# Gates of 128 of 256 tokens scattered by adding transfers instead of built by matmuls, in a one-core decoder step

## What is computed

```
q = (h @ w_q).reshape(C, 8, 2, 128)
s = einsum('cphd,phkd->cphk', q, sub_keys)
s1, i1 = top_k(s[:, :, 0], 16);  s2, i2 = top_k(s[:, :, 1], 16)
cand = s1[..., :, None] + s2[..., None, :]        # 16 x 16
top_s, top_i = top_k(cand, 16)
e = (i1 * 128 + i2) at top_i
g = softmax(top_s)
a = gelu(einsum('cpkd,cd->cpk', u_tab[e], h))
out = einsum('cpk,cpkd->cd', g * a, v_tab[e])
```

## Time and profile before

| | us |
|---|---|
| median of 3 runs | 1083.57 |
| runs | 1078.32, 1083.83, 1083.57 |
| the profiled execution | 1080.47 |
| its span | 1078.8 |

### The profile page before, as it was taken

One profiled execution on the slowest core, in us unless ns is written; L12 is line 12 of the kernel. 1 busy time (PEld: TensorE's weight loads), 2 busy tenths in 40 slices (PEclk: granted clock), 3 DMA queues, 4 the chain that ended last, 5 costly groups with the idle time before them and its releaser, 6 DMA issues.

```text
span 1078.8 us, 23502 instructions
## 1 busy us (share of the span) xinstructions
PE 1054.4 (98%) x7240; PEld 947.7 (88%) x7240; DVE 856.5 (79%) x1952; ACT 553.8 (51%) x1052; POOL 128.1 (12%) x151
## 2 busy tenths in 40 slices
PE   7999998999999999999999999999999999999997
PEld 7997647989999999999999999997788888888865
DVE  5324386698988989888459999987888888888878
ACT  5425475454544444444555555555555555555543
POOL 0344400000001000544000000000201001010100
PEclk9999999999999999999999999999999999999999
DMA  7655932333468766999864444558888888888872
GB/s 278 267 190 186 353 116 107 102 134 131 164 219 288 248 236 225 373 411 413 294 212 122 146 146 141 156 172 314 294 297 284 296 280 295 285 292 289 293 247 93
DMA packets 96248, 253.19 MB, mean 235 GB/s; under 512 B 11424, under 2 KB 44224, under 8 KB 95408
## 3 DMA queue, kind: packets, MB, share of 16 engines
q1 hardware_dynamic: 81840, 196.84, 52.5%
q0 software_dynamic: 14368, 55.87, 14.7%
HBM read 232.60 MB, written 22.12 MB: 236 GB/s over the span
## 4 chain that ended last, share of the span: by engine, by line
PE 81%; DMA 8%; DVE 5%; issue 3%; ACT 2%; SPq 1%; DVEq 0%; POOL 0%; ACTq 0%; POOLq 0%
PE ps L562 13%; PE ps L563 13%; PE ps L564 13%; PE ps L1039 9%; PE ps L1041 9%; PE ps L1040 9%; DMA activations<-u_out 5%; PE ps L1016 5%; DMA a_in<-activations 2%; PE ps L646 1%; DVE w_lo L1437 1%; PE ps L938 1%; ACT w_hi L1097 1%; DMA ring<-in_w_in_dram 1%; DMA vrow<-in_v_dram,expert 0%
## 5 line engine op out<-in xcount | busy, mean ns | idle before, releaser
L1437 DVE TENSOR_TENSOR w_lo<-ring,w_hi 128x512 fp32r<-128x512 f32 (+1 forms) x455 | 388.8, 858 | 124.0 <-ACT w_hi L1097 105.0
L1097 ACT CAST w_hi<-ring 128x512 fp32r<-128x512 f32 (+1 forms) x453 | 341.0, 753 | 96.7 <-PE ps L1041 60.8
L562 PE MATMUL ps<-h_hi,w_hi 128*128 128x256 f32 (+1 forms) x1128 | 330.3, 293 | 0.4 <-issue 0.2
L563 PE MATMUL ps<-h_lo,w_hi 128*128 128x256 f32 (+1 forms) x1128 | 321.1, 285 | 0.0
L564 PE MATMUL ps<-h_hi,w_lo 128*128 128x256 f32 (+1 forms) x1128 | 319.4, 283 | 0.0
L562 PEld LDWEIGHTS ps<-h_hi,w_hi 128*128 128x128 f32 x1128 | 214.9, 191 | 4.0 <-issue 3.2
L563 PEld LDWEIGHTS ps<-h_lo,w_hi 128*128 128x128 f32 x1128 | 214.2, 190 | 0.0
L564 PEld LDWEIGHTS ps<-h_hi,w_lo 128*128 128x128 f32 x1128 | 211.8, 188 | 0.0
L1039 PE MATMUL ps<-w_hi,y_hi 128*128 128x512 f32 x496 | 193.7, 391 | 2.2 <-DVE y_lo L1921 1.9
L1041 PE MATMUL ps<-w_lo,y_hi 128*128 128x512 f32 x496 | 193.0, 389 | 0.0
L1040 PE MATMUL ps<-w_hi,y_lo 128*128 128x512 f32 x496 | 193.0, 389 | 0.0
(11 more groups left out here) (372 smaller groups left out, 1278.6 us busy)
## 6 DMA issues: line engine op xcount, KB each, us to landing
ring<-in_uT_dram SPq DMA_DIRECT2D x128, 512.0 KB
ring<-in_v_dram SPq DMA_DIRECT2D x128, 512.0 KB
activations<-u_out SPq DMA_DIRECT2D x128, 128.0 KB
a_in<-activations SPq DMA_DIRECT2D x124, 128.0 KB, 4.6
ring<-in_w_in_dram SPq DMA_DIRECT2D x22, 512.0 KB
ring<-in_w_q_dram SPq DMA_DIRECT2D x16, 512.0 KB
ks<-in_cache_sb_dram POOLq DMA_DIRECT2D x16, 256.0 KB, 3.2
vs<-in_cache_sb_dram POOLq DMA_DIRECT2D x16, 256.0 KB, 5.5
```

Of the source, the lines that this page charges most:

```text
L562: mm(out, hi, hi_, start=start, stop=False)
L563: mm(out, hi, lo_, start=False, stop=False)
L1097: nc.scalar.copy(w_hi[slot][:, x], ring[:, ring_slot, x]).then_inc(part_hi, 2 if half is None else 1)
L1437: V.tensor_tensor(w_lo[slot][:, x], ring[:, ring_slot, x], w_hi[slot][:, x].bitcast(F32), ALU.subtract).then_inc(part_lo[ring_slot], 2 if ...
```

## The change

It does these things:

- The gates of tokens 0 to 127 no longer come from matmuls. Eight transfers on SP, after three w_out loads, write zeros over an 8 MB table in DRAM (`g_dram`, read as [first index, second index, token]). DVE computes for each of the 128 slots (8 heads x 16) of each token the position (first index x 128 + second index) x 128 + token, and the gate. POOL issues 128 indirect transfers, one for each slot, that add 128 single values (one for each token) to the table, with a wait for all that went before at each 16th. Eight transfers of 1 MB then bring the table into `gates[:, 0]`, each waiting for the one before, and the first for the end of up tile 111, since the buffers of the weights lie there.
- The gates of tokens 128 to 255 are built as before, in 16 up tiles instead of 32 (`U_ALONE` is 112).
- On DVE the lists of the first half are sorted first, then its route, then the samples, then the lists of the second half, four row products, its route, and the other 28 products, with five low parts more after each fourth. On POOL the gathers of u rows stand in groups of four between the scatters; the v gathers stand behind the eight loads.
- `hrow` is added to `sacc` by DVE instead of by PE.
- In front: `ns_turn` ahead of `rms_sums(0)`, five first halves of output tiles instead of four, one low part moved behind the last sums of the LayerNorm; at the end the samples' square root and finish are at other places.

The diff, without the lines that only allocate or assert:

```diff
 
-        U_ALONE = NE - DT // 8
+        U_ALONE = NE - GN // 8
 
...
         OUT_BANK = (4, 5, 6, 7, 0, 1, 2, 3)
-        OUT_DONE = [2 * AT_OUT + 4 + OUT_ORDER.index(c) + 1 if c < 4 else 2 * (AT_OUT + c + 1) for c in range(N_OUT)]
+        OUT_DONE = [2 * AT_OUT + 5 + OUT_ORDER.index(c) + 1 if c < 4 else 2 * (AT_OUT + c + 1) for c in range(N_OUT)]
 
...
                 load(AT_OUT + n, w_out[n])
+            sp.wait_ge(cmp_clear, 1)
+            for q in range(8):
+                sp.dma_start(g_rows[:, 16 * q:16 * (q + 1), :],
+                             spread_out[:, :].unsqueeze(1).to_broadcast([128, 16, 128])).then_inc(cleared, 16)
             sp.wait_ge(ss_pv, 2)
...
             pool.wait_ge(ch_mm, 2)
+            nc.gpsimd.memset(spread_out[:, :], 0.0)
             nc.gpsimd.memset(cvd[:, :], 0.0)
...
             at_slot = lambda k: bass.IndirectOffsetOnAxis(ap=expert[:, k:k + 1], axis=0)
-            pool.wait_ge(ix_ready, 1)
-            for k in range(SLOTS):
-                if k >= 4:
-                    pool.wait_ge(u_dot, k - 3)
-                nc.gpsimd.indirect_dma_start(urow[:, k % 4, :], None, u_rows, at_slot(k)).then_inc(ug_in[k % 4], 16)
+            def gates_out(first, last):
+                for m in range(first, last):
+                    if m and m % TOPK == 0:
+                        pool.wait_ge(spread_in, 16 * m)
+                    nc.gpsimd.indirect_dma_start(
+                        g_dram, bass.IndirectOffsetOnAxis(ap=spread_at[:, m:m + 1], axis=0), spread_out[:, m:m + 1],
+                        None, compute_op=ALU.add).then_inc(spread_in, 16)
+
+            def rows_in(first):
+                for k in range(first, first + 4):
+                    if k >= 4:
+                        pool.wait_ge(u_dot, k - 3)
+                    nc.gpsimd.indirect_dma_start(urow[:, k % 4, :], None, u_rows, at_slot(k)).then_inc(ug_in[k % 4], 16)
+
+            pool.wait_ge(cleared, 16 * 8)
+            pool.wait_ge(spread_ready, 1)
+            for part in range(16):
+                gates_out(8 * part, 8 * part + 8)
+                if part == 1:
+                    pool.wait_ge(ix_ready, 1)
+                    rows_in(0)
+                if part == 2:
+                    rows_in(4)
+                if 4 <= part < 10:
+                    rows_in(8 + 4 * (part - 4))
+            pool.wait_ge(spread_in, 16 * 8 * TOPK)
+            pool.wait_ge(w_mm, 2 * (AT_U + U_ALONE))
+            for q in range(8):
+                if q:
+                    pool.wait_ge(gates_in, 16 * q)
+                pool.dma_start(gates[:, 0, 16 * q:16 * (q + 1), :], g_rows[:, 16 * q:16 * (q + 1), :]).then_inc(gates_in, 16)
             v_rows = v.rearrange("j p d -> (j p) d")
...
             row_in(1, 1, None)
-            pool.wait_ge(g_sb, 4 + DT // 4)
+            pool.wait_ge(g_sb, 4 + GN // 4)
             for m in range(2, SLOTS):
...
                 if u == 7:
-                    rms_sums(0)
                     ns_turn()
...
                     np_values(u - 1)
+                if u == 7:
+                    rms_sums(0)
                 if u == 1:
...
             out_tile(2, range(4))
-            for c in OUT_ORDER[0:4]:
+            out_tile(4, range(4))
+            for c in OUT_ORDER[0:5]:
                 out_tile(c, range(4, KD))
-            for c in range(4, KD):
+            for c in range(5, KD):
                 out_tile(c, range(KD))
...
 
-            pe.wait_ge(rt_pick, 2)
+            pe.wait_ge(rt_pick, 1)
             pe.wait_ge(s_sb, 4 + 16)
...
             for c in range(3):
-                for tt, (t0, n) in enumerate(TOK[0:2]):
-                    ins = nc.tensor.transpose(ps[:, 4 + c, t0:t0 + n], pick[0:n, tt, c, :], ident[0:n, 0:n])
-                ins.then_inc(rt_t, 1)
+                nc.tensor.transpose(ps[:, 4 + c, 0:GN], pick[:, 1, c, :], ident[:, :]).then_inc(rt_t, 1)
             experts_up(U_ALONE // 4 - 1, U_ALONE // 4)
...
             pe.wait_ge(rt_slot, 3)
-            with pe.Fori(0, DT // 32) as i:
+            with pe.Fori(0, GN // 32) as i:
                 for r in range(4):
...
             ins.then_inc(f_mm, 1)
-            pe.wait_ge(g_sb, 4 + DT // 4)
+            pe.wait_ge(g_sb, 4 + GN // 4)
 
...
                     experts_down(r, halves(i, AT_V + r), 4 * i + r + 1)
-            pe.wait_ge(v_acc, SLOTS)
+            pe.wait_ge(v_acc, SLOTS + 1)
             for half in range(2):
                 x = slice(half * 512, (half + 1) * 512)
-                mm(ps[0:32, 4 + half, :], k("fold"), sacc[:, x], start=True, stop=False)
-                ins = mm(ps[0:32, 4 + half, :], ident[0:32, 0:32], hrow[0:32, x], start=False, stop=True)
+                ins = mm(ps[0:32, 4 + half, :], k("fold"), sacc[:, x], start=True, stop=True)
             ins.then_inc(f_mm, 1)
...
                 if u == 7:
-                    act.wait_ge(rm_mm, 1)
-                    deviation(srow[:, :], ps[:, 7, 0:T], 512).then_inc(rm_sd, 1)
                     act.wait_ge(ns_tb, 1)
...
                     nc.scalar.copy(ptcs[:, :], ps[0:NC_, 1, 0:256]).then_inc(ns_pt, 1)
+                    act.wait_ge(rm_mm, 1)
+                    deviation(srow[:, :], ps[:, 7, 0:T], 512).then_inc(rm_sd, 1)
                 np_copy(u)
...
             nc.scalar.copy(hrow[:, :].rearrange("p (a b) -> p a b", b=512), ps[:, 4:6, :]).then_inc(hr_sb, 1)
-            with act.Fori(0, U_ALONE // 4 - 3) as i:
+            with act.Fori(0, 3) as i:
                 for r in range(4):
                     gelu_then_high(i, r, 4)
+            act.wait_ge(rt_exp_in, 1)
+            A(pick[:, 0, 2, :], pick[:, 0, 2, :], ACT.Exp).then_inc(rt_exp, 1)
+            for r in range(4):
+                gelu_then_high(3, r, 4)
+            with act.Fori(4, U_ALONE // 4 - 3) as i:
+                for r in range(4):
+                    gelu_then_high(i, r, 4)
 
...
             A(sgate[:, :], sgate[:, :], ACT.Exp).then_inc(rt_exp, 1)
-            for tt in range(2):
-                A(pick[:, tt, 2, :], pick[:, tt, 2, :], ACT.Exp).then_inc(rt_exp, 1)
+            A(pick[:, 1, 2, :], pick[:, 1, 2, :], ACT.Exp).then_inc(rt_exp, 1)
             for r in range(8):
...
                         act.wait_ge(rt_t, c + 1)
-                        nc.scalar.copy(slotT[:, c, :], ps[:, 4 + c, 0:DT]).then_inc(rt_slot, 1)
+                        nc.scalar.copy(slotT[:, c, :], ps[:, 4 + c, 0:GN]).then_inc(rt_slot, 1)
                     act.wait_ge(u_dot, SLOTS)
...
 
-            with act.Fori(0, DT // 32) as i:
+            with act.Fori(0, GN // 32) as i:
                 for r in range(4):
...
                         act.wait_ge(g_mm, 16 * i + (2 + 4 * r + 2 * half + 2))
-                        nc.scalar.copy(gates[:, :, bass.ds(32 * i + (8 * r + 4 * half), 4)],
+                        nc.scalar.copy(gates[:, 1, :, bass.ds(32 * i + (8 * r + 4 * half), 4)],
                                        ps[:, 4 + (2 * r + half) % 4, :].rearrange("p (t j) -> p j t", j=128)
...
                 highs_down(0, j)
+                if j == NE - LAST - 1:
+                    root(0, slice(0, 32))
             for q in range(LAST):
...
                 high(slot, value, N_W + q, 1)
-                if q == 0:
-                    root(0, slice(0, 32))
             root(1, slice(0, 128))
...
             low_next()
-            low_next()
             residual(6)
...
             into(squ2[:, 0, :], sqb[:, 7, :]).then_inc(ln_q, 1)
+            low_next()
 
...
             pace(0)
-            for c in range(16):
-                dve.wait_ge(s_sb, 4 + c + 1)
-                h, side = 2 * (c % 4) + c // 8, c // 4 % 2
-                top16([(sT[:, tt, c, :], val[:, tt, h, side, :], idx[:, tt, h, side, :]) for tt in range(2)])
-                pace(2, PACE_Q if c < 10 else PACE)
-            top16([(sS[:, q, :], val[:, 2, q // 2, q % 2, :], idx[:, 2, q // 2, q % 2, :]) for q in range(4)])
-            pace(4)
+            def place_of(c):
+                return 2 * (c % 4) + c // 8, c // 4 % 2
+
+            def lists_of(tt, c):
+                h, side = place_of(c)
+                return sT[:, tt, c, :], val[:, tt, h, side, :], idx[:, tt, h, side, :]
+
+            for c in range(0, 16, 2):
+                low_next()
+                dve.wait_ge(s_sb, 4 + c + 2)
+                top16([lists_of(0, c), lists_of(0, c + 1)])
+                low_next()
 
...
 
-            route(2, 2, sgate[:, :])
-            link(V.scalar_tensor_tensor(posf[:, 0:SLOTS], pick[:, 2, 1, 0:SLOTS], 128.0, pick[:, 2, 0, 0:SLOTS],
-                                        ALU.mult, ALU.add))
-            V.tensor_copy(expert[:, :], posf[:, 0:SLOTS]).then_inc(ix_ready, 1)
-            for tt in range(2):
-                route(tt, 8, pick[:, tt, 2, :])
-            dve.wait_ge(hr_sb, 1)
-            for j in range(SLOTS):
-                dve.wait_ge(ug_in[j % 4], 16 * (j // 4 + 1))
```

(72 more changed lines are left out.)

18 lines of the change are left out of this document (13 added, 5 removed).

## The result

The changed kernel takes 1110.8 us (median of 4, 1105.7 to 1121.3) against 1080.9 for the kernel before: ratio 1.028, 95% interval 1.025 to 1.032. Forecast were 1057 us and a range from 1043 to 1090. The profiled execution took 1121.3 us, the longest of the four; its span is 1119.6. In a second series the ratio was 1.022 [1.019, 1.026].

The account below looks back on a forecast made before the run. PE, busy 98% of the span, was taken to bound the kernel. From 1080.5 us, -28.5 - 0.3 - 1.9 - 4.8 + 2 + 9 = -24.5 gave 1056, stated as 1057; whole range 1043 to 1090.

Parts of the forecast that it names:

- Gates' matmuls: PE in the up stage: 64 token pairs fewer at 0.445 us each, 28.5 us less.
- transposes: PE, gates' stage: three of six transposes go, 0.3 us less.
- rival (e): Gates' stage: the 28.5 us are not gained, since DVE can't build the one-hots faster; chance 0.01.
- `hrow` and the tail: End of kernel: hrow's matmul pairs leave PE, 1.9 us; table load and sample's finish spread against a wait, 0.7 us.
- The front: PE before the expert stages: reordered work fills waits and shortens the layer norm's chain; gains 2, 1.3 and 0.8 us.
- The clearing: Zero writes of 8.4 MB queued on SP among w_out loads: about 30 us long, no cost, bounds 0 and 8 us.
- rival (d): The clearing ends after 176 us and holds w_out tiles up to 8 us: 1062 to 1065; chance 0.08.
- The second half's gates: Late up stage: gates of tokens 128 to 255 normalised at 597 where PE wants them at 596, 2 us lost.
- The Pool queue: Scatters at 1.32 us, then loads, delay the first v row; PE waits about 9 us, bounds 0 and 35.
- 48 x S - 54.6: PE's wait behind the Pool queue in us, for S us per scatter; 9 at 1.32, gains used up at 1.84.
- Rival (c): Pool queue: the adding transfers themselves are slow in HBM; 1103 us at 2.3 us per scatter; chance 0.18.
- Rival (b): Pool held by DVE's two-input instructions, 1.5 to 1.6 us a scatter: wait 25 to 35 us, 1072 to 1082; chance 0.15.

Follow-up runs that it names:

- v-row kernel: The changed kernel with the first two gathers of v rows ahead of the table loads, two loads then, one more after every four gathers; 1085.5 us, ratio 1.0034.
- front-and-tail kernel: The kernel before with only the change's small edits in the front and the tail, including hrow added by VectorE; ratio 0.9969.
- four-and-six kernel: The v-row kernel with scatters moved ahead, second-half gates earlier, and four low parts and six scatters between groups instead of five and eight; 1072.0 us, ratio 0.9905.
- half scatters: The changed kernel with each scatter over 64 partitions in place of 128, the gates of 64 tokens left out; 1102.3 us, ratio 1.018.

## Why the prediction was wrong

- **Gates' matmuls, -28.5, transposes, -0.3: right.** In the v-row kernel the up stage ends 18.8 us earlier by itself in spite of a wait of 8.6: 27.4, with a clock of 0.97 in the 50 us behind that wait. PE waits for no one-hot in this kernel or the changed one, so rival (e) is out.
- **`hrow` and the tail, -2.6: right**, 2.3 in the trace of the front-and-tail kernel.
- **The front, -4.1 without the tail: the number was met by luck** (4.1 and 4.5 where the new front runs at full clock). Filled waits, the forecast's mechanism, give 1.0, since each opened another, as the bounds allowed; 3.5 come from the lower clock level that the kernel before shows in this stretch and these profiles don't. The sum has no term for the clock, which in four of thirteen profiles also falls behind the wait for `oT` and takes about 6 us.
- **The clearing, 0: right.** DMA share 1.03, and the same 598 matmuls take no longer; rival (d) is out.
- **The second half's gates, 2 us: 10.0, 6.6 and 8.6 in three profiles.** In the v-row kernel the gates are there at 599.6 (forecast 597) and PE at 591.0 (forecast 596). PE's 596, like the 695 of the v row, leaves out the 4.1 us that the same sum takes off the front. So the hits in time are in part luck: the first scatter at 343 (342.9 in the v-row kernel, 354.3 in the first profile, late with its front) and the last gather at 588 (590.1, 601.7) come 4.5 and 6.7 us later than forecast in the v-row kernel, if counted from the keys' load. The forecast also missed that DVE waits for the last row products' gathers (5.1 us in the first profile). Without scatters 5.4 us are left.
- **The Pool queue, +9: this step failed, by its first factor, the price of a scatter.** I took the gather's 1.32 us for a scatter, because both make 128 descriptors. Behind the last gather 48 scatters take 602.9 to 714.4, less two landing waits of 7.8: 103.7, or 2.16 each. The parts, from the runs: 0.96 for a plain scatter, 0.59 for the addition, 0.30 between instructions, 0.30 of waiting for VectorE. So the gather's price would have held for a plain write; the addition and VectorE, both put at nothing, make up the difference, some 28 and 14 us over 48 scatters. The other factors held: landing waits of 7.8 us for 8, loads 5.8 us apart for 5.8. The formula itself, 48 x S - 54.6, gives 49.1 us at 2.16; the two stops are 52.5. That it fell into two stops the forecast did not have: the first table piece, called not late, was issued at 716 and cost 20.9 by itself.
- **The rivals on this step.** Rival (c), 0.18, had the right formula and at S = 2.3 a time of 1103; the addition does cost more, as it said. But it placed the price in HBM, and the waits on landings stayed at the forecast's 8: the 0.59 us are in GpSimd's own instruction. The reason against it was the gathers' 1.32 us; what decided was the clause behind it, "but they do not add". Rival (b), 0.15, had the interference with VectorE at 0.2 to 0.3 us, near the 0.30 measured, and not the addition; by the formula its 1.5 to 1.6 us a scatter give a wait of 17 to 22 us and not the 25 to 35 written there.

The sum with the measured sizes: -28.8 - 2.3 - 4.3 + 8 + 52.5 is +25, 1106; 2.7 more are PE's slower running behind the two stops, 1109. The medians of the two series are 1111 and 1108. The -4.3 is the front at full clock, which neither profile of the changed kernel had; what its other executions had there no trace shows.

**The part of VectorE.** In the gates' stage I expected DVE's short instructions to leave the scatters alone. They don't. POOL and DVE of the changed kernel:

```profile
644.14 2.01 POOL L548 DMA_INDIRECT gates<-spread_out,spread_at  x1 [0.30 <-issue]
646.46 2.02 POOL L548 DMA_INDIRECT gates<-spread_out,spread_at  x1 [0.31 <-issue]
```

```profile
644.04 0.69 DVE L1481 TENSOR_TENSOR w_lo<-ring,w_hi 128x512 fp32r<-128x512 f32 x1
...
646.36 0.69 DVE L1481 TENSOR_TENSOR w_lo<-ring,w_hi 128x512 fp32r<-128x512 f32 x1
```

Each scatter begins 0.10 us into a half w_lo, which has 0.59 us to run, and lasts 1.55 plus 0.47. The next w_lo is 2.32 us away, two turns of PE; 2.02 and 0.30 are 2.32, so the scatter meets it again, turn after turn. When DVE stands, at 709 to 713, it is 1.55 each. In the whole of the first profile 66 scatters are lengthened that begin while a product of two SBUF tiles runs (53 times a w_lo, 10 times a row product), and 63 of them last 1.55 us plus what the product still has to run less 0.13, to within 0.06. By the same rule the gather at 441.15 of the earlier trace rows comes out: 0.94 + 1.17 - 0.13 = 1.98. A scatter that begins just ahead of a w_lo (609.92, the w_lo 609.93) takes 1.55. The end can be hit as well: in the v-row kernel nine scatters from 667 to 687 us begin beside the one-hots, take 1.87 to 2.02 us and end 0.05 before a w_lo does (673.60 to 675.61, the w_lo 674.97 to 675.66). All this is coincidence in time, many times over; no kernel here took the w_lo away.

The rule that I cited from the Trainium skill, page "SBUF — State Buffer", section "Who interferes with whom", says that the two contend, and the trace agrees; the error was to read it as a matter of how long DVE's instructions are instead of where they lie. The Trainium skill, "DMA: Bandwidth & Descriptors", section "Anatomy of one DMA", calls descriptor generation small, with many to be had before it shows. The half scatters agree as to each descriptor, 0.15 us for 64; but GpSimd is busy 0.96 us for a scatter of 128 values as a write and 1.55 as an addition, and some 1.25 of these do not depend on their number.

**A version that beats both.** The four-and-six kernel is 0.95% faster than the kernel before (ratio 0.987 to 0.994), the front and tail edits alone, which it contains, 0.3% (interval up to 0.9998). Of the 27 us that the scatters would save if free, it keeps 11.

## What to carry to other kernels

Price an operation by a row of the same operation; where there is none, a sum that depends on it 48 times has to be shown at twice the nearest row, and the break-even compared with that. Once one queue has no gap left, reordering its work only moves the wait from one place to another: add up the queue's own time from its first to its last instruction before trying orders. And put what is needed soon (the v rows) ahead of what is needed in portions: that alone was worth 21 to 27 us here. A gain that comes out as forecast is still to be looked up in its place: the front's came mostly from the clock.

## What the runs showed of the hardware

- An indirect scatter of 128 x 4 B keeps GpSimd busy 0.96 us as a write, 1.55 as an addition; the addition with 64 descriptors takes 1.40. Beside it a VectorE product of two SBUF tiles that already runs adds what it has left, less 0.13 us (63 of 66 scatters, first profile).
- Plain 4-byte scatters issued 1.27 us apart hold PE's matmuls up one by one (23.5 us from 340 to 400); four at a time with a wait for the landings do not (0.6), nor do adding scatters, 1.85 us apart or more (0.6).
- The granted clock of one and the same order of instructions was 0.77 in four profiles and 1.00 in others over the same 30 us.
